# A score cluster of the differential mixer issued three chunks later, beside the compression, and a partial sum over the full array

## The reference

```python
p1 = _masked_softmax(jnp.einsum('bhqd,bhkd->bhqk', q1b, k1) * scale, mask)
p2 = _masked_softmax(jnp.einsum('bhqd,bhkd->bhqk', q2b, k2) * scale, mask)
p = p1 - lam * p2
o_b = jnp.einsum('bhqk,bhkd->bhqd', p, v)                 # B: four heads
...
blocks = t[:, widx] + pe                                  # D: 15 blocks of 32 tokens
kc = blocks.reshape(b, nc, NSA_CMP_LEN * d) @ w           # compressed keys, and values alike
```

## Time and profile before

| what | value |
|---|---|
| median of 3 runs (lowest, highest) | 828.03 us (827.93, 828.12) |
| profiled execution, its own time | 828.2 us |
| its span on the core | 826.4 us |
| instructions in the span | 11044 |
| TensorE | 821.6 us busy, 4050 matmuls |
| VectorE, ScalarE, GpSimd | 559.7, 477.8, 293.7 us busy |
| granted TensorE clock | 1.0 in every stretch looked at |

### The profile page before, as it was taken

The page is one execution under the profiler, slowest core; times in us unless marked ns, Lnnn a source line. Parts: engine busy times, 40 slices in busy tenths (PEclk is TensorE's granted clock), DMA queues, the critical chain, the costliest instruction groups (busy, mean ns, idle before and its releaser), DMA issues.

```text
span 826.4 us, 11044 instructions
## 1 busy us (share of the span) xinstructions
PE 821.6 (99%) x4050; PEld 673.7 (82%) x4050; DVE 559.7 (68%) x821; ACT 477.8 (58%) x715; POOL 293.7 (36%) x297
## 2 busy tenths in 40 slices
PE   9999999999999999999999999999999999999998
PEld 5888888888888888888888888888788888888886
DVE  5576889868865666655454688898697666666542
ACT  6886655785465554543457775567844645454441
POOL 0078784404303432320000889653061044323100
PEclk9999999999999999999999999999999999999999
DMA  9745877684558777785565556878745687877652
GB/s 332 271 138 178 222 230 219 182 247 131 203 178 229 199 230 212 223 221 183 167 203 195 162 192 192 224 222 210 223 153 178 206 214 218 230 223 212 215 184 71
DMA packets 119637, 167.76 MB, mean 203 GB/s; under 512 B 56608, under 2 KB 59040, under 8 KB 119328
## 3 DMA queue, kind: packets, MB, share of 16 engines
q1 hardware_dynamic: 119296, 166.79, 66.9%
q10 hardware_dynamic: 288, 0.27, 0.1%
HBM read 153.40 MB, written 1.05 MB: 187 GB/s over the span
## 4 chain that ended last, share of the span: by engine, by line
PE 98%; DMA 1%; issue 0%; SPq 0%; ACT 0%; DVE 0%
PE acc L732 91%; PE att L812 1%; PE att L895 1%; PE att L779 1%; PE att L886 1%; DMA w_raw<-in_w_in 1%; PE att L804 1%; PE acc L812 1%; PE att L853 0%; PE att L869 0%; PE att L908 0%; PE att L972 0%; PE att L963 0%; PE att L854 0%; PE att L839 0%
## 5 line engine op out<-in xcount | busy, mean ns | idle before, releaser
L1234 DVE TENSOR_TENSOR w_lo<-w_raw,w_hi 128x1024 fp32r<-128x1024 f32 (+1 forms) x276 | 365.4, 1337 | 147.1 <-ACT w_hi L996 144.6
L732 PE MATMUL acc<-w_hi,xt 128*128 128x512 f32 (+1 forms) x1728 | 432.3, 392 | 0.5 <-ACT xt L1019 0.3
L996 ACT ACTIVATE w_hi<-w_raw 128x1024 fp32r<-128x1024 f32 (+1 forms) x275 | 286.1, 1051 | 168.7 <-PE acc L732 159.1
L732 PEld LDWEIGHTS acc<-w_hi,xt 128*128 128x128 f32 x1728 | 319.0, 188 | 66.3 <-issue 1.3
L732 PE MATMUL acc<-w_lo,xt 128*128 128x512 f32 (+1 forms) x864 | 229.9, 388 | 0.0
L732 PEld LDWEIGHTS acc<-w_lo,xt 128*128 128x128 f32 x864 | 162.0, 188 | 32.9
L1485 POOL TENSOR_SCALAR small<-small 128x2 f32<-128x2 f32 (+4 forms) x14 | 10.4, 745 | 209.2 <-ACT sq_dump L1096 132.4
L1617 POOL COPY hid_t<-hid_halves_t 128x512 uint16<-128x512 uint16 x44 | 37.7, 885 | 94.3 <-DMA hid_halves_t<-hid_halves 80.0
L1608 POOL COPY hid_halves<-hid 128x512 uint16<-128x512 uint16 x44 | 45.6, 1064 | 65.2 <-DVE hid L1311 65.2
L1625 POOL TENSOR_TENSOR merged<-merged,prod 128x1024 f32<-128x1024 f32 x10 | 32.5, 3250 | 61.2 <-DVE prod L1283 60.3
L732 PE MATMUL acc<-w_hi,ht_hi 128*128 128x512 f32 x176 | 47.7, 390 | 0.0
(11 more groups left out here) (175 smaller groups left out, 723.5 us busy)
## 6 DMA issues: line engine op xcount, KB each, us to landing
w_raw<-in_w_ffn SPq DMA_DIRECT2D x88, 512.0 KB, 4.2
w_raw<-in_w_gate SPq DMA_DIRECT2D x64, 512.0 KB, 3.9
w_raw<-in_w_ffn_down SPq DMA_DIRECT2D x44, 512.0 KB, 4.0
w_raw<-in_w_in SPq DMA_DIRECT2D x39, 512.0 KB, 4.7
w_raw<-in_w_branch SPq DMA_DIRECT2D x16, 512.0 KB, 4.1
w_raw<-in_w_out SPq DMA_DIRECT2D x16, 512.0 KB, 3.3
bg<-in_b_gate SPq DMA_DIRECT2D x8, 512.0 KB, 5.4
w_raw<-in_w_in SPq DMA_DIRECT2D x8, 396.0 KB, 3.4
```

The source lines that it names most:

```text
L732: return pe.matmul(acc[bank0 + t][:, 0:N], x_part[:, k0 + k, t * P:(t + 1) * P], w_part[:, k, 0:N], start=first, stop=last)
L996: act.activation(w_hi[:, n % WR, :, 0:N], w_raw[:, n % RAW, :, 0:N], copy).then_inc(s_hi, 1)
L1234: dve.tensor_tensor(w_lo[:, n % WR, :, 0:N], w_raw[:, n % RAW, :, 0:N], w_hi[:, n % WR, :, 0:N].bitcast(F32), ALU.subtract).then_inc(s_lo, 1)
```

## The change

Mixer B's second score cluster moves from u = 27 to u = 30, and what follows it: `Bp` of heads 2 and 3 from 27 and 29 to 30 and 32, `Bpt` from 29 and 32 to 32 and 34, `Bpv` from 33 and 35 to 35 and 37, `Bo` from 36 to 38. The compression's `ck` and `cv` move from 31 to 30; `cks` stays at 31. And `cks` uses all 128 columns of the constant in place of 16, so that its sum comes out on all 128 rows; ACT still copies 16 of them.

```diff
-    "Bsm": (21, 21, 27, 27), "Bp": (21, 24, 27, 29), "Bpt": (24, 27, 29, 32), "Bpv": (27, 29, 33, 35), "Bo": 36,
+    "Bsm": (21, 21, 30, 30), "Bp": (21, 24, 30, 32), "Bpt": (24, 27, 32, 34), "Bpv": (27, 29, 35, 37), "Bo": 38,
...
-    "cbuild": 29, "ck": 31, "cks": 31, "cv": 31, "kcprep": 32, "kct": 37, "cr": 35, "cs": 39, "cp": 39,
+    "cbuild": 29, "ck": 30, "cks": 31, "cv": 30, "kcprep": 32, "kct": 37, "cr": 35, "cs": 39, "cp": 39,
...
-                            pe.matmul(att[0:16, TP, 0:HD], cst[:, C_REP:C_REP + 16], kpart[:, :], start=True, stop=True
+                            pe.matmul(att[:, TP, 0:HD], cst[:, C_REP:C_REP + P], kpart[:, :], start=True, stop=True
```

## The result

| what | before | after |
|---|---|---|
| median of 5 runs (lowest, highest) | 828.03 us (827.73, 828.41) | 832.04 us (831.56, 832.15) |
| ratio, with its 95% interval | | 1.0046 (1.0032 to 1.0061) |
| profiled execution, its span | 828.2, 826.4 us | 832.1, 830.3 us |
| chunk 26 to chunk 38, first layer | 41.78 us (86.02 to 127.80) | 43.53 us (86.06 to 129.59) |
| the same, second layer | 41.78 us (494.68 to 536.46) | 43.88 us (496.49 to 540.37) |

What follows compares the result with a forecast made beforehand. TensorE's list, busy 99% of the span, was taken as the bound. Per layer 1.3 us of waits less 0.16 of work gave 1.14, for two layers 2.3: 830.3 us predicted, range 828.7 to 832.2.

Steps and rivals of the forecast that it cites:

- two new waits: TensorE waits at the scores, some 0.3 us, and at head 2's transposes in visit 32, 1.0: together 1.3 per layer.
- Slowed splits: Rival, 13%: VectorE's splits take 2.04 us beside GpSimd's copies, not 1.22; visit 34 up to 0.8 late; 831.2 to 832.6.
- TensorE's work, -0.16 us per layer: Junctions around the moved steps on TensorE: 0.11 - 0.17 - 0.10 us, bounds -0.4 and 0.
- the 0.17 us for the way from the four transposes to the scores: Visit 27: price of going from the full array to tiles of 32 rows, 0.53 against 0.36 us, removed.
- The wait at the scores, about 0.3: Visit 30: TensorE waits for VectorE's copy of the values' sum, 0.21 us plus two handoffs.
- ScalarE's chain, +9.11 to the end of the copies: From the compression's start, ScalarE finishes copying the sum of partial keys at +9.11 us; TensorE reaches head 2's transposes at +7.83.
- So the bank decides, not the data: Visit 32: head 2's coefficients are done at +7.49 us, before TensorE's +7.83, so its transposes wait only for ScalarE's copy.
- coefficients of 1.26 us: VectorE's time for a head's coefficients, taken from the profile before (93.83 to 95.09).
- A wait of line 869 for VectorE: Sign of a wrong forecast: head 2's transposes wait for VectorE's coefficients rather than for ScalarE.
- GpSimd's list is not moved past anything: Claim that GpSimd's and SyncE's lists are not moved past anything; no delay was counted for it.
- The four transposes of visit 27 down to 0.36, everything behind them cheaper by 0.27: Visit 27 without the cluster: transposes fall from 0.53 to 0.36 us, and the product behind gets 0.10 cheaper.

Runs made afterwards that it cites:

- visit 27 relieved: Changed kernel with head 2's transposes one chunk later, head 3's coefficients one earlier, head 1's transposes at 29, its product at 31: 828.89 us, 1.0011.

## Why the prediction was right in its direction and too small

Slower was forecast, with TensorE's list as the bound and two new waits as the cause, and that is what happened. But 832.0 lies outside the forecast's own 829.3 to 831.2; the range of 828.7 to 832.2 holds it only because it takes in most of the rival *Slowed splits*. That this rival was priced at just 832.0 is luck: its delay of 0.8 us per layer in visit 34 was some 0.06. By the steps:

- *TensorE's work, -0.16 us per layer: right as far as the runs show.* The scores took the 0.86 us expected; with no second wait, the first layer's loss of 0.61 us leaves -0.15 for the junctions if visit 27's 0.36 is set apart whole, and -0.10 if only its wait of 0.31 is. One term of it was read too high: of the 0.17 us for the way from the four transposes to the scores 0.10 came back (0.53 to 0.43).
- *The wait at the scores, about 0.3: right.* 0.41 and 0.40 us, until VectorE's copy (100.65 + 0.23) was through. The wait row says "issue" in place of VectorE.
- *ScalarE's chain, +9.11 to the end of the copies: right.* They ended at +9.14 (108.32 + 0.30, from 99.48), and the transposes began at +9.24. The terms on the way came as counted too: the first exponential at +4.37 for +4.33, the eighth done at +7.89 for +7.86.
- *"So the bank decides, not the data": failed in the second layer.* It rested on coefficients of 1.26 us, read where none of these copies ran. In their new place they took 2.83 and, in the second layer, 3.24 us (516.11 to 519.35), beside copies that before ran at 104.42 to 107.77, mostly beside VectorE's splits. There the transposes came at +9.58, not +9.11: 0.47 us. A wait of line 869 for VectorE was among the prediction's own signs of being wrong, and it came in this layer. The prediction's statement that GpSimd's list is not moved past anything was true of the list and missed what runs beside it. Its rival *Slowed splits* had VectorE slowed beside GpSimd's copies, which is what happened, but named the wrong instructions: the split it named took 1.30, while the coefficients' L1385 took 1.95 us beside the copies and 0.75 with them held back.
- *The four transposes of visit 27 down to 0.36, everything behind them cheaper by 0.27: failed by 0.36 us in each layer.* This is the largest error; 0.31 of it is the wait that visit 27 relieved shows, 0.05 the transposes. The prediction took the cluster out and asked only what its junctions cost; it did not ask what the cluster had covered, which was ScalarE's copy of `TP`, with 0.88 us to spare before and the cluster 0.86 of that.

Added up, with 1.14 us forecast per layer: first layer 1.14 + 0.36 + 0.13 (9.24 against 9.11) = 1.63 of 1.75; second 1.14 + 0.36 + 0.47 = 1.97 of 2.10. Of the rest, 0.12 and 0.13, about half is the wait in visit 34: 2.79 us from chunk 33 to head 3's transposes in the first layer (111.83 to 114.62) and 2.80 in the second (522.61 to 525.41), where 2.73 was taken. The other half was not followed up.

## What to carry to other kernels

When a step leaves a place, ask what it covered there: list the waits that its neighbours would have if they stood directly behind each other. When a step arrives, look at what the other engines run at that time, not only at its own engine's list. And where two things are late together, taking one away shows nothing: here freeing the bank alone gained nothing, and freeing bank and data together moved the wait to the next tie.

## What was not expected of the hardware

A VectorE instruction on two columns took 0.65 us, and 1.07 in the second layer, beside a GpSimd copy, and 0.22 with the copies held back. In both layers it ended where the copy did (at 106.60, the copy at 106.57; in the second layer at 517.38, the copy at 517.36). The two reciprocals just ahead of it, with one input each, took 0.17 and 0.15 us beside the same copy in the first layer (from 105.75 and 105.83, the copy from 105.41), as with the copies held back. The wider sum of the partial keys (128 columns) passed faster in a visit of its own than the narrow one, 0.13 against 0.22 us between two starts.
